# Order of the experts in the mixture-of-experts stage: all two-unit experts first, instead of a fixed mixture

## What is computed

```
scores = sigmoid(tok @ w_router)
_, idx = top_k(scores + b_router, 4)
wts    = 2.5 * sel / sum(sel)                    # sel: the four scores
gate   = sum over k of wts[:, k] * one_hot(idx[:, k], 32)
a      = silu(tok @ w_eg[e]) * (tok @ w_eu[e])   # for each expert e: 1024 -> 256
routed = sum over e of (a * gate[:, e]) @ w_ed[e]   # 256 -> 1024
y      = routed + (silu(tok @ w_sg) * (tok @ w_su)) @ w_sd
```

## Time and profile before

| what | value |
|---|---|
| time, median of 3 runs (lowest to highest) | 1962.29 us (1958.25 to 1966.35) |
| the profiled execution: its own time | 1963.68 us |
| its span | 1961.9 us |
| TensorE busy | 1691.9 us, 86% of the span |
| VectorE, ScalarE, GpSimd busy | 29%, 21%, 12% |
| bytes moved | 386.15 MB, mean 197 GB/s |
| of these on the queue of the weights | 337.13 MB, 46.3% of the 16 DMA engines' span |

### The profile page before, as it was taken

One profiled execution on the slowest core, in us unless ns is written; L12 is line 12 of the kernel. 1 busy time (PEld: TensorE's weight loads), 2 busy tenths in 40 slices (PEclk: granted clock), 3 DMA queues, 4 the chain that ended last, 5 costly groups with the idle time before them and its releaser, 6 DMA issues. The chain is left out here.

```text
span 1961.9 us, 26742 instructions
## 1 busy us (share of the span) xinstructions
PE 1691.9 (86%) x9308; PEld 1070.6 (55%) x9308; DVE 569.7 (29%) x1305; ACT 413.3 (21%) x850; POOL 229.2 (12%) x186
## 2 busy tenths in 40 slices
PE   4989999999898889679936998999999888968983
PEld 2656556655467645345523665666656764535552
DVE  2055473321112511101122455644211251111112
ACT  2221135431002211111112210255200221111110
POOL 0003010000000113213200002100000012321320
PEclk7998899999998899889968988999999899989996
DMA  9411136577720699979972111321232069997993
GB/s 364 145 53 57 36 91 215 206 248 254 248 108 0 227 321 377 387 277 386 395 266 75 54 44 44 89 78 44 75 123 107 1 232 328 384 378 279 384 382 111
DMA packets 166626, 386.15 MB, mean 197 GB/s; under 512 B 21408, under 2 KB 59296, under 8 KB 166048
## 3 DMA queue, kind: packets, MB, share of 16 engines
q1 hardware_dynamic: 139344, 337.13, 46.3%
q0 software_dynamic: 17568, 25.22, 5.5%
q10 hardware_dynamic: 9584, 22.10, 3.0%
HBM read 372.32 MB, written 33.03 MB: 207 GB/s over the span
## 5 line engine op out<-in xcount | busy, mean ns | idle before, releaser
L721 PE MATMUL ab<-hT,slot 128*128 128x384 f32 x1344 | 460.3, 499 | 39.0 <-PEq L749 25.7
L721 PEld LDWEIGHTS ab<-hT,slot 128*128 128x128 f32 x1344 | 259.0, 195 | 224.7 <-issue 62.6
L721 PE MATMUL vb<-slot,arena 128*64 128x256 f32 x2560 | 311.9, 399 | 67.1 <-PEq L771 67.0
L721 PEld LDWEIGHTS vb<-slot,arena 128*64 128x64 f32 x2560 | 206.6, 143 | 154.6 <-issue 90.4
L721 PE MATMUL vb<-arena 64*64 64x16 f32 (+3 forms) x1272 | 157.3, 354 | 28.5 <-PEq L730 25.0
L625 POOL DMA_INDIRECT expert_sums<-arena,sum_index x76 | 119.1, 1567 | 368.5 <-POOLq L624 195.4
L1856 DVE SCALAR_TENSOR_TENSOR arena<-vb,unit_gate,arena 128x128 f32<-128x128 f32 x80 | 28.1, 351 | 429.5 <-DVEq L1855 429.5
L721 PEld LDWEIGHTS vb<-arena 64*64 64x64 f32 (+2 forms) x1272 | 84.8, 182 | 73.6 <-issue 71.0
L721 PE MATMUL ab<-slot,hT 128*128 128x384 f32 (+1 forms) x384 | 119.7, 467 | 0.0
L755 PEld LDWEIGHTS ab<-con,arena 128*128 128x128 f32 x560 | 61.2, 141 | 91.9 <-issue 90.4
L721 PE MATMUL vb<-yT,slot 128*128 128x384 f32 x288 | 103.0, 486 | 0.0
(11 more groups left out here) (240 smaller groups left out, 1587.2 us busy)
## 6 DMA issues: line engine op xcount, KB each, us to landing
slot<-in_w_up SPq DMA_DIRECT2D x64, 2048.0 KB
slot<-in_w_mod SPq DMA_DIRECT2D x24, 2048.0 KB
slot<-in_w_mgate SPq DMA_DIRECT2D x32, 1024.0 KB
nat<-in_w_down SPq DMA_DIRECT2D x32, 1024.0 KB, 17.2
slot<-in_w_in SPq DMA_DIRECT2D x10, 2048.0 KB
arena<-in_w_down SPq DMA_DIRECT2D x16, 1024.0 KB, 17.9
hT<-in_w_down SPq DMA_DIRECT2D x16, 1024.0 KB, 14.4
slot<-in_w_out SPq DMA_DIRECT2D x4, 2048.0 KB
```

What stands on the lines that cost most here:

```text
L721: i = nc.tensor.matmul(out, lhsT, rhs, start=start, stop=stop, skip_group_check=True)
```

## The change

Only the order of the kinds changes. Before it is f h h f h three times and then f h h h. After it is seven f and then twelve h:

```
 FULL = 8
 EXTRA = 18
-PAIR_KINDS = "fhhfh" * 3 + "fhhh"
+PAIR_KINDS = "f" * 7 + "h" * 12
```

## The result

The changed kernel takes 1993.33 us (median of 4 runs, 1991.55 to 1995.87), the kernel before 1961.49 us beside it (4 runs, 1958.25 to 1966.35). The ratio is 1.0161, with a 95% interval of 1.0136 to 1.0186: slower by 27 to 37 us. The profiled execution has a span of 1990.3 us against 1961.9, 28.4 us more.

A forecast was written before the change was run, and what follows sets the result against it. DMA and TensorE were taken as nearly level in the expert stages. Layers of -9.0 + 22.6 - 2 = +11.6 and -10.8 + 22.6 - 2 = +9.8 us gave +21.4, so 1984 us, range 1970 to 1998.

The forecast's parts named there:

- its own price: Behind the loop, upper bound: a job more costs 9.5 us instead of 7.5, 6 us a layer more, +33.
- What bounds the stage: Expert stages: DMA limits one-unit jobs (8.6 us against TensorE's 6.6), TensorE limits two-unit jobs (13.2 against 9.8).
- First, ahead of the loop: Units 0 to 17: jobs fall from 14 to 11, TensorE's pace holds; gains 9.0 and 10.8 us.
- Second, the loop: Between units 17 and 18: the wait on unit 17's add stays, or is up to 2 us shorter.
- Third, behind the loop: Units 18 to 37: three more loads cost 22.6 us a layer, less 2 us of room.
- The 2 us of room: Behind the loop: spare DMA time and the sooner add take 2 us off each layer's cost.
- How long the three loaded jobs last: Behind the loop: units 18 to 20 or 21 at full pace, then one unit every 8.6 us.
- (B): Behind the loop: DMA keeps up and TensorE's pace holds everywhere, only the gain is left, 1938 us; chance 0.05.
- (C): Behind the loop: DMA had some 8 us of room a layer, or jobs cost 8.2 us; some 1971; chance 0.15.
- (D): Behind the loop: units wait about 2 us each and the clock falls; about 2020 if for whole units; chance 0.06.

The follow-up runs named there:

- half loads: Two of four pieces of each planned expert's up weights loaded: changed order 1925.70 us, order of before 1928.64; ratios to the kernel before 0.9836 and 0.9835.
- the two finer orders: Kernel before's 14 and 17 jobs, mixed but starting with a one-unit pair: 1954.60 us; the same with a two-unit expert last: 1957.61 us.
- the reversed order: Changed kernel turned round, twelve one-unit pairs first, seven two-unit experts last (18 jobs ahead of the loop, 13 behind): 1985.38 us, ratio 1.0138 to before.
- the coarse orders: Kernel before's job counts, unmixed within each side of the loop: two-unit experts first 1991.35 us (1.0146), one-unit experts first 1989.84 us (1.0137).

## Why the prediction came out as it did

The time lies in the forecast range (1993 in 1970 to 1998), the sign is right, and the forecast is low: 1984 against 1993, or +21.4 against +28.4 us in the profile. The medians are 31.8 us apart, within the interval of the ratio. Part of the nearness is luck. The two stages, which the forecast adds up, grew by 33.2 us and not by 21.4; 4.7 us came off outside them, of which the forecast knew nothing. The upper bound is also not what its own price gives: 9.5 us for a job makes +33.4, so 1996. By the forecast's own steps:

**What bounds the stage** was right. The forecast prices were 8.6 us of DMA for a one-unit job and 13.2 us of TensorE for a two-unit one; the late units of the changed kernel come 8.6 us apart in the first layer, and (1947.17 - 1841.84) / 12 = 8.8 in the second, where unit 25 starts at 1841.84. The half loads show that nothing but weights separates the two orders ahead of and behind the loop.

**First, ahead of the loop**: forecast gains 9.0 and 10.8 us, measured 8.9 and 10.8. The forecast DMA share of 0.8 to 0.9 there was 0.88 to 0.94 from 700 to 800 us.

**Second, the loop**: it was forecast as long as before, or up to 2 us shorter because the add would land sooner. It is 0.2 us shorter in one layer and 2.7 us longer in the other. The wait for the add did not shrink, it grew: 11.85 and 12.49 us where it was 10.79 and 10.93. The second layer (before, then changed):

```profile
1768.57 1.94 PE L755 MATMUL ab<-con,merged 128*128 128x128 f32 x8 [10.93 <-PEq L730]
...
1772.82 1.94 PE L755 MATMUL ab<-con,merged 128*128 128x128 f32 x8 [12.49 <-PEq L730]
```

The other part is the loop's own up matmuls, which took 9.77 and 8.66 us before and 8.47 and 9.80 us after. Over the 11 kernels of the experiments the loop stretch lies between 38.4 and 42.8 us; half loads have 39.7 to 41.5 too. The kernel before and the two finer orders have the shortest, 38.4 to 39.6 us, but the reversed order has 39.3 in one layer as well. With one profile for each kernel the 2.7 us can't be put down to the change, and what spreads the stretch stays open.

**Third, behind the loop**, is the step that was mis-sized: 20.6 us for a layer, measured 25.7 and 24.6. Two terms of it, from the queues over the whole stretch from unit 18 to unit 37 in the first layer. Before:

```profile
q1 hardware_dynamic: 11424, 44.31, 88.5%
q0 software_dynamic: 3600, 3.68, 14.0%
```

Changed:

```profile
q1 hardware_dynamic: 14049, 54.20, 89.4%
q0 software_dynamic: 3600, 4.05, 12.8%
```

The packets of the gathers and adds are the same 3600, as forecast. But their share of time went from 0.140 x 126.2 = 17.7 to 0.128 x 151.9 = 19.4 us: 0.37 MB more. That fits the plan: behind the loop the six units of ranks 12 to 17 now stand in place of the six of ranks 4 to 6, and an expert split over two units may well have fewer tokens in each. The counts of tokens are not in the trace, so this is not shown. The two shares add up to 1.022 and 1.025 over such a stretch and not to the 1.036 of the best 80 us, so three loads cost 3 x 7.79 / 1.022 = 22.9 us. The weights' queue also moved 9.89 MB more and not 9.44. The other 0.45 MB may be of the next layer's loads, which follow in the same queue; that is a guess. 22.9 + 1.7 + 0.45 / 0.404 = 25.7 us, what was measured. In the second layer the shares add up to 0.991 in both kernels, and the same two terms give 3 x 7.79 / 0.991 + 1.8 = 25.4 us. The queue moved 9.31 MB more there, 0.13 less than three jobs, so the whole account gives 25.1 us for 24.6 measured (before, then changed):

```profile
q1 hardware_dynamic: 11125, 43.74, 84.3%
q0 software_dynamic: 3600, 4.01, 14.8%
```

```profile
q1 hardware_dynamic: 13492, 53.05, 85.5%
q0 software_dynamic: 3600, 4.39, 13.6%
```

**The 2 us of room** that I took off did not exist as a saving: with it gone and the terms above, the two stages would have been forecast at 25.7 - 9.0 and 25.4 - 10.8, +31.3 in all, where they measured +33.2. The loop's 2.5 us, less the 0.8 by which this is too high for the second stage, make up the rest. I had read a share of 0.99 in one window as time that could be used; the changed kernel has 0.99 from 860 to 880 us too. I had also read the end of the stage from the last unit alone, a wait of 2.4 and 1.8 us. By the whole stretch the kernel before was already 2.4 and 6.7 us behind TensorE's own pace there.

**How long the three loaded jobs last** was too short in the forecast, by units: it said units 18 to 20 or 21 at full pace, and it was units 18 to 24. That has no part in the end time, which the queue sets.

**The rivals.** (B), the DMA keeps up, is excluded by the late units. (C), the DMA has room, too: there was none. (D): of the 26 units from unit 25 on, both layers together, 11 took 5.1 to 5.8 us for their up matmuls and the others 3.67, but the down matmuls and transposes did not slow, and the units kept the queue's pace; the page shows a mean granted clock of 0.92 as before. The figure of the Trainium skill, page "HBM Reference", section "Specifications (TRN2)", of about 358 GB/s for a core would give an estimate of 26.4 us for three loads, near the 25.7 by chance only. The same section says that this is what each of two cores gets when both stream, and that a core alone measures well above it. Here one core runs, and the trace agrees with that: it moved 395 to 400 GB/s in the windows above.

A reason that the forecast did not have, though its sum is not hurt by it: it counted jobs on each side of the loop, and the coarse orders show that this is not the rule. What matters is whether the queue is kept busy in each stretch as long as the tiles can cover. The count priced the changed kernel well because its two sides are the simple cases: TensorE's own pace ahead of the loop, and one-unit experts alone behind it.

## What to carry to other kernels

When jobs of equal bytes and unequal compute share a ring of a few tiles, mix them so that within the depth of the ring load time and compute time balance; a run of the long ones idles the queue for good, a run of the short ones starves TensorE, wherever it stands. Begin with short jobs, for the first tile then comes free sooner; here that was worth 0.2%. To price such a change, find which of the two limits holds at the last job, and multiply the loads moved by the share that one load takes over that whole stretch, not by the best window's rate; halving the loads in both orders then tells in two runs whether it is the loads at all.

## What the runs showed that I had not expected

The DMA share of a saturated stretch adds up to 1.02 to 1.04 in the first layer, but to 0.99 from unit 18 to unit 37 in the second, in both kernels, and there the share falls off at the end. The windows of 5 us of the changed kernel end so, while the weights of unit 37, which starts at 1947.17, have not all landed (last columns: granted clock, DMA share, GB/s):

```profile
1930.00:1935.00 5.00, 4.20 (x24) 3.11 (x26) 0.00 (x0) 0.00 (x0) 0.84 (x1) 0.66 1.03 393
1935.00:1940.00 5.00, 3.90 (x28) 2.11 (x26) 1.04 (x2) 1.15 (x3) 0.39 (x1) 1.00 0.80 311
1940.00:1945.00 5.00, 5.00 (x41) 3.02 (x37) 0.35 (x1) 0.28 (x1) 1.16 (x1) 1.00 0.52 170
```

A share of 0.52 while a load is awaited suggests that some of the 16 engines have no more to do for it while others still work. Here the last up weights, with only their down weights behind them, were awaited until some 7 to 12 us after the mean share began to fall. That the engines lag each other by different amounts is an inference from these shares; it wasn't tried by itself.
